# Transposes and pooled products issued inside contractions, output weights loaded in the second block, one reduction per peak

## What is computed

```
h = rmsnorm(x, g_pre);  proj = h @ w_in
u, gate_a, q, k, v, qi, ki, wi, gate_b = split(proj)
# pool branch: four groups of 128 channels, windows 2/4/8/16
d = mean_window(u) - u;  y_a = (d @ w_pool[group]) * pool_scale
# indexer: which 256 keys a query may see
score = sum_h wi[h] * relu(qi[h] @ ki.T) * INDEX_SCALE     # 8 heads of 32
sel = top_k(score, 256)
# attention over the selected keys (8 heads of 64, 2 kv heads), with a relative bias
out = concat(y_a * silu(gate_a), attention * silu(gate_b)) @ w_out
y = x + rmsnorm(out, g_post)
```

## Time and profile before

| | |
|---|---|
| three runs | 1782.69 us median (1781.55 to 1783.21) |
| the profiled execution | 1783.91 us, its span 1781.8 us |
| PE busy | 1592.5 us, 89% |
| DVE busy | 1245.7 us, 70% |
| ACT busy | 899.8 us, 51% |
| POOL busy | 486.8 us, 27% |
| mean granted TensorE clock | 0.965 |

### The profile page before, as it was taken

One profiled execution on the slowest core, in us unless ns is written; L12 is line 12 of the kernel. 1 busy time (PEld: TensorE's weight loads), 2 busy tenths in 40 slices (PEclk: granted clock), 3 DMA queues, 4 the chain that ended last, 5 costly groups with the idle time before them and its releaser, 6 DMA issues.

```text
span 1781.8 us, 17814 instructions
## 1 busy us (share of the span) xinstructions
PE 1592.5 (89%) x5144; PEld 880.3 (49%) x5191; DVE 1245.7 (70%) x2988; ACT 899.8 (51%) x1684; POOL 486.8 (27%) x384
## 2 busy tenths in 40 slices
PE   6999899989998988876788888999999999999996
PEld 3555555555555766654334444444444444455542
DVE  5412556657777888984437999999999999884213
ACT  3112323333334334541269988988888786423331
POOL 0111211121112112121333434343423332323342
PEclk9999899989999989988799999999999999999999
DMA  9322322211111110038332322221120120100101
GB/s 336 63 54 47 79 61 51 64 64 55 45 55 47 39 56 31 34 115 244 90 87 69 105 69 77 79 61 49 52 83 30 43 60 23 37 30 18 36 24 47
DMA packets 91978, 120.76 MB, mean 68 GB/s; under 512 B 17149, under 2 KB 63805, under 8 KB 91498
## 3 DMA queue, kind: packets, MB, share of 16 engines
q1 hardware_dynamic: 90218, 114.91, 20.7%
q10 hardware_dynamic: 1664, 4.72, 2.2%
HBM read 76.06 MB, written 43.54 MB: 67 GB/s over the span
## 4 chain that ended last, share of the span: by engine, by line
DVE 20%; PE 20%; issue 6%; ACT 4%; another core or an unknown queue 2%; POOL 1%; SPq 0%; DMA 0%; POOLq 0%; DVEq 0%; ACTq 0%
DVE above L329 7%; PE wide L1593 6%; PE wide L1609 5%; DVE max_junk L1672 3%; PE bank L1573 2%; PE bank L1575 2%; PE bank L1574 2%; ACT act_junk L1504 1%; PE bank L1578 1%; POOL E L1463 1%; DVE den L1687 1%; PE bank L1560 1%; DVE reach L367 1%; DVE S L363 1%
## 5 line engine op out<-in xcount | busy, mean ns | idle before, releaser
L906 PE MATMUL bank<-hT,home 128*128 128x512 f32 (+2 forms) x1280 | 487.5, 524 | 10.0 <-DVE sga L1114 7.9
L1463 POOL TENSOR_TENSOR E<-E,home 128x512 f32<-128x512 f32 x174 | 262.2, 1511 | 476.9 <-ACT E L1537 476.7
L906 PEld LDWEIGHTS bank<-hT,home 128*128 128x128 f32 x1280 | 242.6, 196 | 181.0 <-issue 157.3
L1537 ACT ACTIVATE E<-bank 128x512 f32<-128x512 f32 x290 | 171.4, 591 | 280.6 <-PE bank L1578 221.3
L1593 PE MATMUL wide<-E,home 128*128 128x512 f32 x544 | 284.4, 605 | 12.4 <-POOL E L1463 9.8
L886 ACT ACTIVATE relu<-wide 128x1024 f32<-128x1024 f32 (+7 forms) x192 | 153.5, 802 | 193.2 <-PE wide L921 115.9
L1152 DVE SCALAR_TENSOR_TENSOR S<-relu,wi,S 128x1024 f32<-128x1024 f32 (+7 forms) x168 | 175.6, 1045 | 71.7 <-ACT relu L886 61.7
L1672 DVE CUSTOM_DVE_ANT_0 max_junk<-bank,mask 128x512 bf16<-128x512 f32 (+3 forms) x230 | 137.1, 615 | 83.4 <-PE bank L1560 66.0
L1573 PE MATMUL bank<-qh,k 128*128 128x512 f32 x272 | 160.8, 591 | 15.7 <-DMA ql<-q_low_scratch 10.7
L1560 PE MATMUL bank<-k,qh 128*128 128x512 f32 (+3 forms) x214 | 139.7, 675 | 31.5 <-DVE mxp L1672 19.5
L1609 PE MATMUL wide<-home 128*128 128x512 f32 x272 | 141.2, 610 | 24.3 <-ACT osb L1530 22.5
(11 more groups left out here) (198 smaller groups left out, 2328.4 us busy)
## 6 DMA issues: line engine op xcount, KB each, us to landing
qh<-q_high_scratch SPq DMA_DIRECT2D x34, 256.0 KB, 4.1
xs<-x_prompt SPq DMA_DIRECT2D x16, 512.0 KB, 3.8
home<-w_in SPq DMA_DIRECT2D x16, 512.0 KB, 10.5
xr<-x_prompt SPq DMA_DIRECT2D x16, 512.0 KB, 4.3
y_prompt<-osb SPq DMA_DIRECT2D x16, 512.0 KB, 3.0
ql<-q_low_scratch SPq DMA_DIRECT2D x30, 256.0 KB, 4.9
s_scratch<-S SPq DMA_DIRECT2D x11, 512.0 KB, 2.6
gb<-gb_scratch SPq DMA_DIRECT2D x17, 256.0 KB, 4.7
```

The source lines that it names most:

```text
L906: mm = pe.matmul(out, stationary(c), moving(c), start=(c == 0), stop=(c == DC - 1))
L1463: pool.tensor_tensor(E[:, k % 4], E[:, k % 4], EB[:, kv * GRP:(kv + 1) * GRP, off:off + P], ALU.mult)\
L1537: act.activation(E[:, k % 4], banks[2 + k % 2][:].rearrange("p (j n) -> p j n", j=GRP), ACT.Exp).then_inc(fl_free, 1)
```

## The change

Steps `TR`, `CK` and `PL` are no longer put into the list on their own. They go into a queue `short`, and `project` takes up to two of them into the next contraction, spaced among the scores (`aside` issues them). `settle` puts out what is left before the remaining scores of a tile. The functions of the steps are otherwise the same, moved from the PE loop into `aside`. The peak of a chunk is one reduction with the absolute value applied. Both halves of the output weights are loaded in the second block, behind the load of mask 3.

```diff
     def project(step, left):
         k = -(-len(pending) // left) if left > 0 else 0
-        inside[step] = [pending.pop(0) for _ in range(min(k, len(pending), 2 * DC if step[0] == "TM" else DC))]
-        steps.extend(inside[step])
+        pieces = [pending.pop(0) for _ in range(min(k, len(pending), 2 * DC if step[0] == "TM" else DC))]
+        aside = [short.pop(0) for _ in range(min(len(short), 2))]
+        for i, piece in enumerate(aside):
+            pieces.insert((i + 1) * (len(pieces) + len(aside) - i) // (len(aside) + 1) if pieces else i, piece)
+        inside[step] = pieces
+        steps.extend(pieces)
         steps.append(step)
...
     def pool_part():
-        while differences:
-            steps.append(("PL", *differences.pop(0)))
         while windows:
-            differences.append(windows.pop(0))
-            steps.append(("PD", *differences[-1]))
+            steps.append(("PD", *windows[0]))
+            short.append(("PL", *windows.pop(0)))
+
+    def transposes(t):
+        short.extend(("TR", t, part) for part in range(3))
+
+    def settle():
+        while short:
+            steps.append(short.pop(0))
...
-                if j < 3:
-                    steps.append(("TR", t, j))
                 if j == 0:
+                    transposes(t)
...
                     if cached:
-                        steps.append(("CK", t - 4))
+                        short.append(("CK", t - 4))
                     if last:
+                        settle()
                         spread(100)
...
-                                score(*piece)
+                                if piece[0] == "I":
+                                    score(*piece)
+                                else:
+                                    aside(*piece)
...
-                        dve.tensor_reduce(small[:, 0:1], row, AX.X, ALU.min).then_inc(dve_chain, 1)
-                        dve.tensor_reduce(small[:, 1:2], row, AX.X, ALU.max).then_inc(dve_chain, 1)
-                        n += 2
-                        dve.wait_ge(dve_chain, n)
-                        dve.scalar_tensor_tensor(peak[:, c:c + 1], small[:, 0:1], -1.0, small[:, 1:2], ALU.mult, ALU.max)\
-                           .then_inc(dve_chain, 1)
+                        dve.tensor_reduce(peak[:, c:c + 1], row, AX.X, ALU.max, apply_absolute_value=True).then_inc(dve_chain, 1)
...
                     load_mask(t + 3)
+                    if t == 0:
+                        for i in range(2):
+                            sp.dma_start(home[:, (8 + 4 * i) * GROUP:(12 + 4 * i) * GROUP],
+                                         A["w_out"][:, 4 * i * GROUP:4 * (i + 1) * GROUP]).then_inc(wout_in, 16)
```

More of the change, by code:

```diff
@@ L255, in build @@
         home = sb(ctx, "home", [P, 16 * GROUP + DC * TMW], F32)
-        loaded = {name: ctx.enter_context(nc.semaphore(name)) for name in ("eb_in", "v_in", "wout_in", "S_in0")}
+        loaded = {name: ctx.enter_context(nc.semaphore(name)) for name in ("eb_in", "v_in", "S_in0")}
         unit = sb(ctx, "unit", [P, NT], F32)
@@ L923, in score, with aside @@
                     mm.then_inc(fi_full, 1)
+                def aside(*s):
+                    if s[0] == "TR":
+                        _, t, part = s
+                        o = tm_order[t]
+                        bank = fd_bank(s)
+                        pe.wait_ge(split_done, 6 * (o + 1))
+                        if part:
+                            for h in range(4):
+                                tr = pe.transpose(bank[0:3 * DI, h * P:(h + 1) * P], qs[:, 4 * part - 4 + h, :],
+                                                  identf[:])
+                            tr.then_inc(fd_full, 1)
+                            return
+                        for kv in range(NKV):
+                            pe.transpose(bank[:, kv * P:(kv + 1) * P], kparts[:, kv].rearrange("p a d -> p (a d)"),
+                                         identf[:])
+                        pe.transpose(bank[0:3 * DI, 2 * P:3 * P], ks[:], identf[:]).then_inc(fd_full, 1)
+                    elif s[0] == "CK":
+                        bank = fd_bank(s)
+                        pe.wait_ge(ck_split, s[1] + 1)
+                        for kv in range(NKV):
+                            tr = pe.transpose(bank[:, kv * P:(kv + 1) * P],
+                                              ckparts[:, kv].rearrange("p a d -> p (a d)"), identf[:])
+                        tr = pe.transpose(bank[0:3 * DI, 2 * P:3 * P], ksc[:], identf[:])
+                        tr.then_inc(fd_full, 1)
+                    elif s[0] == "PL":
+                        b, g = s[1:]
+                        T = width(b)
+                        bank = fd_bank(s)
+                        pe.wait_ge(small_in, 48)
+                        pe.wait_ge(d_ready, pool_order[b, g] + 1)
+                        fin = win[:, g % 2, UOFF:]
+                        if b == len(BLOCKS) - 1:
+                            pe.matmul(bank[:, 2 * P:T], wpool[:, g, :], fin[:, 2 * P + UOFF:2 * P + UOFF + DEC], start=True,
+                                      stop=True)
+                            T = 2 * P
+                        pe.matmul(bank[:, 0:T], wpool[:, g, :], fin[:, 0:T], start=True, stop=True).then_inc(fd_full, 1)
                 pe.wait_ge(bias_in, 32)
@@ L1305, in phase2 @@
         osb = sb(st, "osb", [P, 2, D], F32)
-        eb_in, v_in, wout_in = (loaded[n] for n in ("eb_in", "v_in", "wout_in"))
+        eb_in, v_in = loaded["eb_in"], loaded["v_in"]
+        wout_in = sem("wout_in")
         qh_in = [sem(f"qh_in{i}") for i in range(3)]
```

48 lines of the change are left out of this document (5 added, 43 removed).

## The result

The changed kernel takes 1761.8 us (median of four runs, 1758.7 to 1766.9) against 1783.0 us before (1781.6 to 1786.0): a ratio of 0.9877, 95% interval 0.9861 to 0.9893. Measured again, beside the last experiments, it took 1759.3 us against 1783.4 us: 0.9866 (0.9848 to 0.9883). Forecast were 1762.7 us and a range of 1752 to 1773.

What follows compares the result with a forecast made beforehand. TensorE was taken to set the pace up to 560 us, VectorE from 682 to 762 us. Terms 14.9 + 6.9 - 2.3 + 0.5 = 20.0 us gave 1762.7 us for the median, range 1752 to 1773 us.

Steps and rivals of the forecast that it cites:

- Bank-3 waits up to 560 us: TensorE's waits for bank 3 from 40 to 560 us all go: 14.9 us gained, bounds 0 and 14.9.
- the rival of no change: Gaps close, but VectorE takes back what TensorE wins before 560 us: 1782.7 us, chance 0.03.
- Bank-3 waits after 560 us: TensorE's 11.1 us of waits go, but VectorE is late there anyway: 0 gained, bounds 0 and 11.1.
- The rival that took all 11.1 us: The larger rival: TensorE's waits after 560 us count after all, gain 31.1 us, 1751.6 us; chance 0.13.
- One pass per peak: One reduction per peak saves VectorE time in tiles 11 to 14: 6.9 us gained, bounds 1.2 and 6.9.
- Tile 16: Transposes between GA 3's scores delay the gate near the first block's end: net -2.3 us, bounds +1.35 and -5.8.
- Output weights: Loading both halves in the second block eases the first block's last stores a little: +0.5 us, bounds 0 and 2.
- tile 15's first peak: Its shorter reduction on VectorE gives back 1.35 us of the 3.6 us lost behind tile 16's gate.
- the 0.8 us inside GB 0: Estimated further loss where tile 16's last transposes and pooled product stand ahead of GB 0's second score: 0.8 us.
- The slower one: Two bank-3 users in one contraction make TensorE wait for ACT in all 17 tiles: 1794.4 us, chance 0.04.
- The smaller one: Tiles 12 to 15 each pay tile 16's 3.6 us: 1777.1 us, or 1769.9 at half that; chance 0.18.
- The rule on swings of the clock: TensorE's micro-idles between matmul groups swing its clock, so closing gaps returns clock; the prediction counted nothing for it.

Runs made afterwards that it cites:

- the place inside alone: Changed kernel with two reductions per peak and the old place of the output weights, leaving only the placing inside contractions: 1773.2 us, ratio 0.9941.
- Tile 16's transposes by themselves: Changed kernel with tile 16's transposes standing between contractions again as before, all else inside: 1759.5 us, ratio 0.9869.
- both changes together: Changed kernel with tile 16's transposes between contractions and the pooled product of U 2 in the next contraction: 1762.3 us, ratio 0.9884.
- with the product later: Changed kernel with the pooled product of U 2 put into the next token-major contraction in tile 16's run-up: 1764.8 us, ratio 0.9889.

## Why the prediction was right, and where not

The time was forecast within 1 us of the first median and 3.4 us of the second, and the mechanism of each large term shows. That the sum came so near is in part luck: smaller terms were off by 1 to 2 us, and not all the same way. The terms, by the ruler, with the 1.15 and 1.54 us of the profile of before taken off:

**Bank-3 waits up to 560 us: 14.9 forecast.** The changed kernel gains 16.57 - 1.15 = 15.4 us up to the 12th gate, 0.7 of it the peaks' own by the kernel with the peaks alone; 18 of the 19 waits, 14.2 us, lie before that gate. But the term was taken as independent of the peaks, and it is not: alone it is worth 12.5 us. The step that failed is the one under the rival of no change, that VectorE's 57.17 of 100 us left it too idle to take anything back. A mean over 100 us hid one place, near 431 us, where a relu was late; in the whole change the one-pass peak covers it.

**Bank-3 waits after 560 us: 0 forecast.** Nearly right. With the edit alone 2.6 us are gained from the 12th to the 18th gate, but 0.7 of it is the last wait of the term above, and 0.8 the wait at 572 us: there TensorE still sets the pace, and the border at 560 us was drawn one wait too early. Behind the 13th gate 0.75 us are left of it. The rival that took all 11.1 us falls.

**One pass per peak: 6.9 forecast.** Of it 5.7 us fall between the 12th and the 18th gate (the two of tiles 11 and 12, both of tile 13, the first of tile 14), and the edit alone gives 5.2 there. With both edits 7.30 - 0.39 = 6.9 us are gained there, less than 5.2 + 2.6. From the 12th to the 13th gate the gain is that of the place inside; from the 13th to the 18th the whole change gains 4.9 us (18.80 at the 13th), the peaks alone 5.2 (1.95 at the 13th) and the place inside alone 0.75. VectorE sets that stage, as the prediction has it, and there TensorE's edit adds nothing to that of the peaks.

**Tile 16: -2.3 forecast.** From the 18th to the 20th gate the terms of the prediction make 1.18 (tile 14's second peak) - 2.8 = -1.6 us, and -1.54 was measured. The number was right by luck, with half its cause missing: the 1.18 us do not show where the peaks are changed alone (0.9 us lost there, above), and a second wait makes part of the loss. Where the prediction says of POOL's differences that they are wanted 0.86 us earlier, "so I take no wait", it looked only at products that go into a contraction. `settle` puts the product of `U 2` out right behind its difference, and TensorE waits 1.78 us for POOL. Tile 16's transposes by themselves, with the rest kept, account for 1.0 us; only both changes together give the 3.0 us back.

**Output weights: +0.5 forecast.** Not to be told from nothing by the whole runs. The two halves did not take 16.6 us each: in the changed kernel they landed in 9.7 us (median).

**After the 20th gate** the terms left (1.35 of tile 15's first peak, the 0.8 us inside GB 0, 0.5 of the weights) make 1.05 us, and 2.28 and 2.45 us were measured, 0.9 us of it seen with the weights alone too. In the first profile 0.8 us lie in the wait for the first queries (11.60 and 10.84 us) and 0.7 us in TensorE's busy time (49.30 and 48.58 us); the rest was not traced. As the clock moved this stretch by 2 us in other versions, a sum to the microsecond can't be expected of it.

The parts measured by themselves make 7.0 + 10.5 + 0.4 = 17.9 us, the whole 21.9 us (0.0123 of 1783) with an interval of about 3 us on either side. That fits the 2.9 us near the 10th gate which only both edits together keep, but the intervals alone would not show it.

**The rivals.** The slower one was real as a mechanism: two users of bank 3 in one contraction wait 0.92 us a time (11.0 us by 12) if nothing lies between them. The spacing in `project` is what keeps it away. The smaller one, tiles 12 to 15 paying what tile 16 pays, does not show: from the 12th to the 18th gate the change gains, and the one new wait of transposes there is 1.1 us.

**The clock.** The rule on swings of the clock (the Trainium skill, "TensorE: Matmul & The Clock Gate", section "A second HAM failure mode: psum-queue depth-cycling") would have given back clock with the gaps closed. From 60 to 545 us the granted clock is 0.98 in the changed kernel:

```profile
60.00:545.00 485.00, 469.19 (x1485) 263.19 (x1485) 254.92 (x719) 157.37 (x295) 84.05 (x77) 0.98 0.22 58
```

and 0.98 before, with 457.99 us of TensorE's work. The closed gaps of 0.7 to 0.8 us gave the waiting time itself and, to the two digits of the view, no clock. The lower clock was seen behind longer waits, of 2.17 and 2.62 us, above, but not behind every long one: in the changed kernel eight transposes took 1.06 us after a wait of 3.77 us (186.39 us) and 1.94 us after one of 3.47 us (359.33 us).

## What to carry to other kernels

Where several short users share one PSUM bank, look in the timeline for two of them side by side, and put other work of the length of the copy between them; whether that work is a contraction's inside or a whole contraction made no difference here. Of two late waits in series, removing one mostly makes the other longer: 1.0 and 0.7 us alone, 3.0 us together, and even of that the clock took back part before the block ended. And a ruler inside the program, one instruction that every version issues in the same order, shows a microsecond where whole runs scatter by several; how well it repeats has to be seen from two profiles of the same work, here 0.06 us in one pair and 1.5 us in the other.

## What the runs showed of the hardware

The same waits at the start of the program do not always bring the same clock. In the changed kernel TensorE's first waits, by its timeline, are these:

```profile
30.86 1.06 PE L984 MATMUL bank<-identf,xs 128*128 128x128 f32 x8 [0.96 <-ACT hT L801]
33.58 1.85 PE L984 MATMUL bank<-identf,xs 128*128 128x128 f32 x8 [1.66 <-DVE xs L1053]
```

and in the second profile of the same program:

```profile
31.20 1.06 PE L984 MATMUL bank<-identf,xs 128*128 128x128 f32 x8 [0.96 <-ACT hT L801]
33.92 1.09 PE L984 MATMUL bank<-identf,xs 128*128 128x128 f32 x8 [1.66 <-DVE xs L1053]
```

After waits of the same 0.96 and 1.66 us the same eight transposes took 1.85 us in one and 1.09 us in the other; the clock granted from 20 to 60 us is 0.91 in the first and 1.00 in the second, and the first gate comes at 61.09 and 58.55 us. Before, it was the luckier case (1.00, first gate at 56.82).

Whole runs go with the mean granted clock: with the product later, 1756.0 us at 0.967 and 1765.1 us at 0.957, for the same program on the same chip. That scatter of 9 us is larger than any single edit to the late stage of the first block.
